# A table of constants that places an expert's tokens six rows apart in a mixture-of-experts layer (one Trainium2 core)

## The reference: what is computed

```python
scores = sigmoid(h @ w_router)                     # 512 tokens x 64 experts
_, top_idx = top_k(scores + router_bias, 8)        # eight experts for each token
gates = normalised scores of those eight, times 2.5
out = x1 + swiglu_shared(h) + sum over e of gates[:, e] * swiglu_e(h)
```

## Time and profile before

| what | us |
|---|---|
| median of 3 runs | 1210.72 |
| lowest and highest | 1209.78, 1212.47 |
| profiled execution, its own time | 1210.36 |
| its span | 1208.4 |
| busy: TensorE, VectorE, ScalarE, GpSimd | 1152.7, 732.4, 572.0, 289.1 |

### The profile page before, as it was taken

One profiled execution on the slowest core, in us unless ns is written; L12 is line 12 of the kernel. 1 busy time (PEld: TensorE's weight loads), 2 busy tenths in 40 slices (PEclk: granted clock), 3 DMA queues, 4 the chain that ended last, 5 costly groups with the idle time before them and its releaser, 6 DMA issues.

```text
span 1208.4 us, 17315 instructions
## 1 busy us (share of the span) xinstructions
PE 1152.7 (95%) x5426; PEld 788.7 (65%) x5426; DVE 732.4 (61%) x1317; ACT 572.0 (47%) x1026; POOL 289.1 (24%) x293
## 2 busy tenths in 40 slices
PE   8999999999999999999999999999999999999994
PEld 5889877777774674566666666566556655665662
DVE  5443466578735445566666766666676666666651
ACT  5434374443434221265555555555555455545552
POOL 0221011000000001132333333333333433343231
PEclk6999999999999999999999999999999999999997
DMA  5333222424130736499999999999999999999951
GB/s 177 122 106 105 71 71 71 139 71 122 60 134 1 280 142 274 148 372 336 346 337 347 341 341 330 346 330 341 331 341 333 339 329 340 331 337 331 340 186 25
DMA packets 65605, 284.63 MB, mean 236 GB/s; under 512 B 12515, under 2 KB 15083, under 8 KB 40604
## 3 DMA queue, kind: packets, MB, share of 16 engines
q1 hardware_dynamic: 51228, 250.50, 56.6%
q0 software_dynamic: 14336, 33.59, 11.6%
HBM read 271.40 MB, written 29.42 MB: 249 GB/s over the span
## 4 chain that ended last, share of the span: by engine, by line
PE 55%; DMA 30%; DVE 6%; issue 3%; ACT 3%; SPq 1%; POOL 1%; ACTq 0%; DVEq 0%
DMA arena_x<-in_w_up_e 29%; PE bank L1472 19%; PE bank L1636 9%; PE bank L1642 7%; PE bank L1656 6%; PE bank L1421 3%; PE bank L1629 2%; PE bank L1615 2%; PE bank L1670 1%; DVE w_lo L969 1%; PE bank L1611 1%; ACT gu_parts L858 1%; ACT arena L729 1%; DMA arena<-in_w_out 1%; PE bank L1526 1%
## 5 line engine op out<-in xcount | busy, mean ns | idle before, releaser
L555 POOL TENSOR_TENSOR turn<-minus_half 16x1 f32<-16x1 f32 x128 | 113.8, 889 | 463.0 <-DMA out<-arena,idxs 391.8
L1642 PE MATMUL bank<-gu_parts,xT_parts 128*96 128x512 f32 x768 | 214.0, 427 | 0.0
L1656 PE MATMUL bank<-w_lo 128*96 128x512 f32 (+1 forms) x816 | 205.8, 401 | 3.9 <-issue 2.9
L1642 PEld LDWEIGHTS bank<-gu_parts,xT_parts 128*96 128x96 f32 x768 | 124.1, 162 | 78.8 <-issue 34.1
L1656 PEld LDWEIGHTS bank<-w_lo 128*96 128x96 f32 (+1 forms) x816 | 131.1, 167 | 51.3 <-issue 3.6
L1268 DVE TENSOR_TENSOR gu_parts<-arena_x,gu_parts 128x1024 fp32r<-128x1024 f32 x64 | 78.2, 1221 | 107.9 <-ACT gu_parts L858 107.4
L1268 DVE TENSOR_TENSOR gu_parts<-arena,gu_parts 128x1024 fp32r<-128x1024 f32 x64 | 78.0, 1220 | 104.6 <-ACT gu_parts L858 104.6
L858 ACT ACTIVATE gu_parts<-arena_x 128x1024 fp32r<-128x1024 f32 x64 | 67.5, 1054 | 132.7 <-DMA arena_x<-in_w_up_e 91.4
L1636 PE MATMUL bank<-arena_x,arena 128*96 128x512 f32 x256 | 116.7, 599 | 12.8 <-DVE arena L1259 12.7
L1472 PE MATMUL bank<-w_hi,hT_hi 128*128 128x512 f32 (+1 forms) x320 | 125.9, 394 | 2.3 <-DVE w_lo L969 1.5
L1636 PE MATMUL bank<-arena 128*96 128x512 f32 x256 | 117.0, 600 | 11.1 <-DVE arena L1259 11.1
(11 more groups left out here) (189 smaller groups left out, 1819.3 us busy)
## 6 DMA issues: line engine op xcount, KB each, us to landing
arena<-in_w_gate_e SPq DMA_DIRECT2D x32, 1024.0 KB, 28.8
arena<-in_w_up_e SPq DMA_DIRECT2D x32, 1024.0 KB, 32.3
arena<-in_w_down_e SPq DMA_DIRECT2D x32, 1024.0 KB, 26.9
arena_x<-in_w_gate_e SPq DMA_DIRECT2D x32, 1024.0 KB, 28.8
arena_x<-in_w_up_e SPq DMA_DIRECT2D x32, 1024.0 KB, 32.1
arena_x<-in_w_down_e SPq DMA_DIRECT2D x32, 1024.0 KB, 27.1
arena<-in_w_in SPq DMA_DIRECT2D x14, 1024.0 KB, 5.4
arena<-in_w_gate SPq DMA_DIRECT2D x8, 1024.0 KB, 6.1
```

The source lines that it names most:

```text
L555: nc.gpsimd.tensor_tensor(turn[:], minus_half[0:16, 0:1], minus_half[0:16, 0:1], ALU.add).then_inc(turns, 1)
L1642: last = nc.tensor.matmul(out_, a[n][:, j, :], b[:, :, j, :], start=False, stop=(j == PLAIN - 1 and i == 2))
L1656: last = nc.tensor.matmul(psY[h][0:rows, :], midT[n][a][:, j, 0:rows], w[b][:, j, h * 512:(h + 1) * 512], start=(j == 0 and k == 0), stop= ...
```

## The change

A constant DMA_ENGINES = 16 is added, and the first 96 of the columns that `iota_b` is copied from hold another order of the numbers 0 to 95:

```diff
--- before.py
+++ after.py
@@ -40,6 +40,7 @@
 MASKED = -1e30
 NEVER = -3e38
 SLOTS = 96
+DMA_ENGINES = 16
 WARM_UP = 56
 NO_TOKEN = 1024
 SEQ = 512
@@ -1794,6 +1795,7 @@
     c = np.zeros((P, 4 * P + tiles + 1 + rounds), np.float32)
     c[:, 0:P] = np.eye(P)
     c[:, P:2 * P] = np.arange(P)[None]
+    c[:, P:P + SLOTS] = np.arange(SLOTS).reshape(SLOTS // DMA_ENGINES, DMA_ENGINES).T.reshape(-1)[None]
     c[:, 2 * P:3 * P] = np.triu(np.ones((P, P)))
     c[:, 3 * P:4 * P] = np.triu(np.full((P, P), MASKED), 1)
     c[:, 4 * P:4 * P + tiles] = np.arange(tiles)[None] * P - NO_TOKEN
```

## The result

The changed kernel takes 1176.17 us (median of 4 runs, 1175.43 to 1178.29) where the kernel before takes 1211.12 us (4 runs, 1209.78 to 1212.47). The ratio is 0.9714, with a 95% interval of 0.9697 to 0.9732: 35 us, where 31 were forecast. In later runs of the kernel before (1209.1 to 1209.3 us) against a table with the same effect (1176.05 us, second experiment) the gain is 33 us. The profiled execution took 1175.43 us, its span 1173.3.

A forecast was written before the change was run, and what follows sets the result against it. TensorE bounds the first stretch at 10.26 us a step, late weight loads the second at 11.00. Loop -31.0, last scatter -0.5, jitter +0.5 give -31.0 us off the 1210.72 median: 1179.7 us, range 1176 to 1198.

The forecast's parts named there:

- What bounds the kernel: Expert loop: TensorE's pace, 10.26 us a step to 692.0 us, then late weight loads, 11.00 us over 42 steps.
- Which DMA engine finishes last: Gathers and scatters: blocks of six rows per engine; ten engines with six rows delay every weight load, five have none.
- a share near 1.00 after the change: Sign of being right: while the first gather moves alone, DMA share near 1.00 instead of 0.68, in a shorter time.
- The even load: DMA time per expert after the change: between 9.70 and 10.70 us, taken at 10.4, so TensorE's 10.26 is late next.
- The rival of a partial gain: Expert loop: even load costs 10.70 to 10.9 us; at 10.8, 13.5 us given back, 1193 us; chance 0.12.
- the shared limit: Rival: engines wait for memory, not each other; even load still needs 11.0 us, time stays 1210.7; chance 0.07.
- slower: Rival: where gather and weights overlap, sixteen engines moving rows lose more rate; 11.35 us an expert, 1225 us; chance 0.06.
- The sum: Whole kernel: -31.0 - 0.5 + 0.5 = -31.0 us, taken off the median of 1210.72 us.
- The loop's term: Second stretch of the expert loop: 42 steps at 10.26 us instead of 461.9 us in all, saving 31.0 us.
- The last scatter: End of the kernel: lands sooner with fewer rows on its busiest engines; 0 to 1.7 us saved, taken at 0.5.
- steps that jitter: Expert loop: an allowance of 0.5 us set against the saving.
- GpSimd's loop: Scatter issue after the previous landing: tied to TensorE's step, not in front of it, with more room after the change.

The follow-up runs named there:

- second experiment: Against the kernel before, ranks 4b to 4b+3 go to block b's first four rows, ranks 64 and up to its last two: 1176.05 us, ratio 0.9724.

## Why the prediction was right

*What bounds the kernel.* Right: two paces, TensorE's 10.26 us and behind the slack the loads' 11.00. The run with a lighter TensorE shows it directly, since there the kernel before hardly gains.

*Which DMA engine finishes last.* Right: blocks of six rows, and the fullest decides. The dose shows it: four filled rows a block (for 38 of the 64 experts, more for the others) give 1176 us, five 1181, six 1201 to 1209, and rows dealt to engines one by one would have made the order of before even already. One full block in sixteen gives 1194 to 1195. But one of the prediction's rows did not bear the weight I put on it. I took the share of 0.68 of the first gather alone as a sign of 11 busy engines and expected a share near 1.00 after the change. Over a microsecond it is 0.72, and near 1.00 only over 0.3 us in the middle:

```profile
478.00:479.00 1.00, 1.00 (x4) 0.52 (x3) 0.00 (x0) 0.00 (x0) 0.00 (x0) 1.00 0.72 238
478.50:478.80 0.30, 0.30 (x2) 0.11 (x1) 0.00 (x0) 0.00 (x0) 0.00 (x0) 1.00 0.97 396
```

In the changed kernel the packets under way at one time rise from about 6 after 0.15 us to 16 after 0.6 us, so the mean share of such a short transfer says little of how many engines have rows. The single packets of that first gather say it outright. It has 62 rows of 4096 bytes and 50 packets of 4 bytes, which fits 34 skipped rows and 16 closing packets. Before, 35 of the 4-byte packets start within 0.11 us of the first packet: as many as five engines with six skipped rows and a closing packet each have. Five more follow by 0.66 us (the block with two rows: four skipped and one closing), then about ten packets are under way at a time, and the ten last closing packets start at 1.35 to 1.77 us. In the changed kernel all 50 start between 0.84 and 1.34 us. With block 15 alone full, 49 start by 1.16 us and the last one at 1.89, with a single packet under way from 1.2 us on. The rows at the end of a gather in the loop, 0.68 and 0.69, were the ones to argue from. In twenty windows of one microsecond, from 880 to 900 us, the share lies between 0.63 and 1.10 before, and between 0.96 and 1.09 in the changed kernel. The lowest window of the twenty, before:

```profile
884.00:885.00 1.00, 1.00 (x5) 0.65 (x4) 0.38 (x1) 0.00 (x0) 0.84 (x2) 1.00 0.63 209
```

and after:

```profile
881.00:882.00 1.00, 1.00 (x6) 0.72 (x5) 0.00 (x0) 0.00 (x0) 0.88 (x1) 1.00 0.96 328
```

The same holds for the loop as a whole. Of the 550 windows of one microsecond between 560 and 690 and between 700 and 1120 us, 34 have a share under 0.80 before, the lowest 0.55; in the changed kernel none has, and the lowest is 0.88.

*The even load.* Bounds 9.70 and 10.70, taken at 10.4; measured at 10.31 with the lighter TensorE once the loads are late, and at 10.26 + 0.10 = 10.36 by the shrinking slack of the changed kernel. It was sized right. A growing landing time gives more than the step behind the slack wherever both can be read: 11.4 us against 11.00 before, 10.6 against 10.51 with five a block, 11.2 against 10.70 with one full block, by the landing time of w_down_e. So the prediction's "about 11.4 us" for the last engine is more than the step that its loads allow; why, no run shows. Also, the four rows an engine that the prediction counted on hold only for experts of up to 64 tokens. The consequence, that TensorE is late next, holds by a narrow margin: the loads alone are 0.05 to 0.10 us a step slower, and only the slack left over hides it to the end of the loop. The rival of a partial gain needed more than 10.7 and is out; so are the shared limit, since the rate rose to 359 and to 367 GB/s, and slower. The figure of about 358 GB/s a core that the Trainium skill gives ("DMA: Bandwidth & Descriptors", section "Where 436 GB/s comes from") is therefore no limit for this core as it ran here: 367 GB/s over 480 us, by the bytes that the queues move, lie above it, without the accumulate's second access.

*The sum.* The loop's term was 31.0 and measured 31.0 us. The last scatter was put at 0.5 and lands 0.5 sooner. The 0.5 us set against it for steps that jitter did not come. What no term had, 3.6 of the 35.1 us between the two profiled executions, is the start (2.7) and the last product (0.9), where the granted clocks differ. That is luck of the executions and not of the change's making. The median of 1176.17 us lies at the very end of a range that began at 1176. The clock differs between executions of one kernel too: the changed kernel's run with its granted clock at 0.985, as in the profiled one of before, took 1178.29 us, 32.1 below 1210.36.

*GpSimd's loop.* As expected, it does not hold up the step of 10.26 us, but it is closer to it than the prediction says. Each scatter still waits for the landing of the one before: between 745 and 1145 us the operation on `turn` waits for it 36 times before and 38 times after, 234.7 and 234.0 us in all, and the next scatter is issued 1.5 us (median) after that landing in the changed kernel. ScalarE waited once, 0.6 us, for a scatter in the changed kernel, and 16 times where TensorE was made lighter with the changed table; there, up to 734 us, this loop goes along with steps of 9.69 us, 0.6 under TensorE's.

## What to carry to other kernels

The gathers and scatters here are cut into fixed blocks of six rows, one to a DMA engine, and the engine with the fullest block sets when the weights beside them land. If some rows of such a transfer are skipped, spread the skipped ones over all blocks; a table of constants can be enough, and it costs no instruction. Look for it where loads land late while the mean DMA share is a few hundredths under 1, and read the short stretches: 0.69 in one of them said more than 0.97 over 455 us, and the single packets of one gather more than either.

## What the runs showed of the hardware that I had not expected

- A full block costs even when it is the only one: 10.70 us a step with one of sixteen, 11.00 with ten.
- Which five engines are free matters by 0.7 to 0.8%, 1200.6 to 1209.3 us, with the same number of full blocks. The cause is open.
- With TensorE busy for 414 and 440 of the 480 us from 600 us on, the granted clock came to 0.94 and 0.96 on the mean, so it was at 1.2 GHz for 55 and 38 of them and at 2.4 GHz for the rest. Before the change, with 432 of 455 us busy, it stayed at 1.00, which is 2.4 GHz.
- The mean DMA share can read 1.02, so a share of 0.98 is not two hundredths from full.
